# Expert blocks of 64 rows in one stationary tile, and the first two projection tiles of each norm multiplied together

## The reference, cut to what matters

```python
for l in range(2):                              # first stage
    xn = rms_norm(h, norm_mix[l]);  proj = xn @ w_in[l]
    ...                                         # recurrence and attention
    h = h + mix @ w_out[l]
    xn = rms_norm(h, norm_ffn[l]);  gu = xn @ w_ffn_in[l]
    h = h + (silu(gu[..., :D_FF]) * gu[..., D_FF:]) @ w_ffn_out[l]

h = rms_norm(x, g_mix) @ w_in                   # second stage
...
x = x + cross_attention(rms_norm(x, g_cross), ...)
hm = rms_norm(x, g_ffn)                         # [512, 1024]
group = argmax(hm @ w_group);  top 2 of the 8 experts of that group per token
for each expert e (of 32), rows xb routed to it:          # 1024 assignments in all
    yb = (silu(xb @ w_gate[e]) * (xb @ w_up[e])) @ w_down[e]   # 1024 -> 512 -> 1024
out = rms_norm(x + sum of a token's two yb * weight, g_final)
```

## Time and profile before

| | |
|---|---|
| time, median of 3 runs | 2981.32 us (2975.47 to 2982.77) |
| profiled execution, own time | 2980.58 us |
| its span | 2978.8 us |
| mean granted TensorE clock | 0.951 of full speed |
| PE busy | 2772.9 us, 93% |
| DVE / ACT / POOL busy | 1587.5 / 956.2 / 1142.2 us |
| DMA | 373.35 MB, mean 125 GB/s |

### The profile page before, as it was taken

One profiled execution on the slowest core, in us unless ns is written; L12 is line 12 of the kernel. 1 busy time (PEld: TensorE's weight loads), 2 busy tenths in 40 slices (PEclk: granted clock), 3 DMA queues, 4 the chain that ended last, 5 costly groups with the idle time before them and its releaser, 6 DMA issues.

```text
span 2978.8 us, 38117 instructions
## 1 busy us (share of the span) xinstructions
PE 2772.9 (93%) x12974; PEld 2209.5 (74%) x12974; DVE 1587.5 (53%) x2172; ACT 956.2 (32%) x1468; POOL 1142.2 (38%) x768
## 2 busy tenths in 40 slices
PE   6989899999998898999999999999889699999994
PEld 4768777887867787778878787875666488888883
DVE  4772664122355845641223433025644699999995
ACT  4322322110023313211110121122112477777775
POOL 4752016666757610066666563610250011111110
PEclk9999899999999998999999999969996899999997
DMA  3213002332322120023323222300131399999995
GB/s 130 66 36 93 1 22 85 99 98 85 92 72 65 49 71 29 1 85 99 96 88 115 78 88 82 106 29 1 38 117 44 124 356 363 356 371 367 364 361 192
DMA packets 82375, 373.35 MB, mean 125 GB/s; under 512 B 15440, under 2 KB 15568, under 8 KB 57552
## 3 DMA queue, kind: packets, MB, share of 16 engines
q1 hardware_dynamic: 71888, 360.23, 35.0%
q0 software_dynamic: 9504, 8.42, 0.9%
q10 hardware_dynamic: 864, 3.15, 0.3%
HBM read 376.97 MB, written 20.97 MB: 134 GB/s over the span
## 4 chain that ended last, share of the span: by engine, by line
PE 83%; DVE 8%; issue 3%; POOL 2%; ACT 2%; DMA 1%; DVEq 0%; ACTq 0%; SPq 0%; POOLq 0%
PE PS L1779 21%; PE PS L1780 20%; PE PS L1781 20%; PE PS L2126 6%; PE PS L2149 4%; PE PS L1893 2%; PE PS L2140 2%; PE PS L2086 2%; PE PS L1845 1%; PE PS L2204 1%; POOL arena L579 1%; POOL arena L578 1%; PE PS L1832 1%; DVE arena L1109 1%; DVE xl L1039 1%
## 5 line engine op out<-in xcount | busy, mean ns | idle before, releaser
L555 POOL TENSOR_SCALAR whi<-ring 128x1024 fp32r<-128x1024 f32 x260 | 291.8, 1122 | 1177.6 <-PE PS L1781 958.8
L558 POOL TENSOR_TENSOR wlo<-ring,whi 128x1024 fp32r<-128x1024 f32 x260 | 657.5, 2529 | 21.7
L1779 PE MATMUL PS<-xh,whi 128*128 128x512 f32 x1312 | 519.9, 396 | 15.1 <-POOL wlo L558 7.1
L1781 PE MATMUL PS<-xh,wlo 128*128 128x512 f32 x1312 | 512.4, 391 | 0.0
L1780 PE MATMUL PS<-xl,whi 128*128 128x512 f32 x1312 | 512.1, 390 | 0.0
L1779 PEld LDWEIGHTS PS<-xh,whi 128*128 128x128 f32 x1312 | 247.7, 189 | 71.6 <-issue 10.6
L1542 DVE TENSOR_TENSOR arena_r<-arena,arena_r 128x1024 fp32r<-128x1024 f32 x256 | 296.3, 1218 | 1.1 <-ACT arena_r L947 1.1
L1780 PEld LDWEIGHTS PS<-xl,whi 128*128 128x128 f32 x1312 | 247.9, 189 | 53.7 <-issue 2.9
L1781 PEld LDWEIGHTS PS<-xh,wlo 128*128 128x128 f32 x1312 | 247.2, 188 | 52.4
L947 ACT ACTIVATE arena_r<-arena 128x1024 fp32r<-128x1024 f32 x256 | 253.2, 1056 | 46.2 <-DMA arena<-w_gate 45.3
L1779 PE MATMUL PS<-xs,whi 128*128 128x512 f32 x560 | 232.2, 415 | 17.4 <-DVE xs L1217 10.1
(11 more groups left out here) (387 smaller groups left out, 4779.9 us busy)
## 6 DMA issues: line engine op xcount, KB each, us to landing
ring<-ring_w SPq DMA_DIRECT2D x280, 512.0 KB, 3.5
arena<-w_gate SPq DMA_DIRECT2D x64, 1024.0 KB, 6.8
arena<-w_up SPq DMA_DIRECT2D x64, 1024.0 KB, 6.8
arena<-w_down SPq DMA_DIRECT2D x64, 1024.0 KB, 6.7
arena<-y_dram SPq DMA_DIRECT2D x8, 512.0 KB, 7.0
xT<-xT_in SPq DMA_DIRECT2D x1, 2048.0 KB, 8.5
out<-arena SPq DMA_DIRECT2D x4, 512.0 KB, 2.6
arena<-memT_in SPq DMA_DIRECT2D x1, 1024.0 KB, 7.4
```

What stands on the lines that cost most here:

```text
L555: nc.gpsimd.tensor_scalar(whi[:, t % 2, :], ring[:, t % RING, :], 1.0, 0.0, ALU.mult, ALU.add).then_inc(sems["whi"], 1)
L558: nc.gpsimd.tensor_tensor(wlo[:, t % RING, :], ring[:, t % RING, :], whi[:, t % 2, :], ALU.subtract).then_inc(sems["split"], 1)
L1779: mm(out, a[0], b[0], start=start, stop=False)
L1781: return mm(out, a[1], b[0], start=False, stop=stop)
```

## The change

**Experts.** A block has `TB` = 64 rows; the number of overflow blocks goes from 8 to 16. `xgT` holds the high parts of the 64 transposed rows in columns 0 to 63 and their low parts in 64 to 127 of one stationary tile. A gate or up chunk is multiplied by two matmuls: that tile by the high part and by the low part of the weight; row r of the output then holds what came from the high part of row r, row 64 + r what came from its low part. ACT copies the two banks to `gsb` and `usb`. `turn_gu` takes the place of `turn_h`: eight plain float32 matmuls with a 128x64 matrix `fold` (ones at r and 64 + r) as the moving operand, which transpose and add the two halves. Silu and the product then work on 128x256 (`silu`, `hidden`). `down` has 64 stationary columns; for the first two quarters it does the three products as before, for the last two one plain float32 matmul per 512 columns, on the loaded floats, with no high and low part. The ACT and DVE orders of a block are changed to fit.

**Behind each norm.** `first_pair` replaces the waiting form of `feature_major`: it waits for the splits of both tiles and for the second chunk of `xh`, then per chunk multiplies both tiles by `xh` (four matmuls), then per chunk both by `xl` (two). In `late_norm` ACT makes the eight `xh` chunks first and the eight squares after them, and PE's sum of the squares moves from behind the second tile to behind the third.

**Routing** is adapted to 64-row blocks: two compare-and-add steps become one comparison against seven limits, the table has 50 blocks instead of 42, and the search for the expert of an overflow block goes over 16 instead of 8.

```diff
-OVER = 7
+TB = 64
+OVER = 15
...
+        xgT = [xh[:, 2 * u:2 * u + 2, :].rearrange("p a b -> p (a b)").rearrange("p (a b) -> p a b", b=P)
+               for u in range(2)]
...
@@ late_norm (ACT)
                     nc.scalar.activation(xh[:, c, :], xT[:, c, :], ACT.Identity, scale=lcol[:, C_FFN + c:C_FFN + c + 1]
                                          ).then_inc(sems["xh"], 1)
+                for c in range(KO):
                     nc.scalar.activation(sq8[:, c, :], xT[:, c, :], ACT.Square).then_inc(sems["sq"], 1)
...
@@ routing (DVE)
-            jj = E_[:, 0:8].unsqueeze(2).broadcast_to([P, 8, NEXP])
+            jj = E_[:, 0:16].unsqueeze(2).broadcast_to([P, 16, NEXP])
...
@@ projections (PE)
+            def first_pair(l, bank, t, high, low):
+                for j in range(2):
+                    pe.wait_ge(sems["split"], nth("split", l, t + j + 1))
                 for c in range(KO):
-                    pe.wait_ge(sems["xn"], nth("xn", l, (wait if wait_low is None else wait_low) + c + 1))
-                    ins = mm(out, whi[:, t % 2, c * P:c * P + P], xl[:, c, :], start=False, stop=(c == 7))
+                    pe.wait_ge(sems["xh"], nth("xh", l, high + max(c, 1) + 1))
+                    for j in range(2):
+                        for w in weights(t + j, slice(c * P, c * P + P)):
+                            mm(PS[:, bank + j, :], w, xh[:, c, :], start=(c == 0 and w.name == whi.name), stop=False)
+                for c in range(KO):
+                    pe.wait_ge(sems["xn"], nth("xn", l, low + c + 1))
+                    for j in range(2):
+                        ins = mm(PS[:, bank + j, :], whi[:, (t + j) % 2, c * P:c * P + P], xl[:, c, :],
+                                 start=False, stop=(c == 7))
+                        if c == 7:
+                            ins.then_inc(sems["tile"], 1)
...
@@ experts (PE)
-                        ins = mm3(PS[:, bank, :], [x[:, c, :] for x in xgT[u % 2]],
-                                  (high(w, k)[:, of], low(w, k)[:, of]),
-                                  start=(c == 0), stop=(c == 7))
+                        mm(PS[:, bank, :], xgT[u % 2][:, c, :], high(w, k)[:, of], start=(c == 0), stop=False)
+                        ins = mm(PS[:, bank, :], xgT[u % 2][:, c, :], low(w, k)[:, of], start=False, stop=(c == 7))
...
+                for j, buf in enumerate((gsb, usb)):
+                    for c in range(4):
+                        ins = mm(PS[:, 4, (4 * j + c) * TB:(4 * j + c) * TB + TB], buf[:, c * P:c * P + P], fold,
+                                 start=True, stop=True)
...
+                        if k < SPLIT_D:
+                            ins = mm3(out, [x[:, k, :] for x in hTs], (high("D", k)[:, of], low("D", k)[:, of]),
+                                      start=(k == 0), stop=False)
+                        else:
+                            ins = mm(out, hT[:, k, :], loaded("D", k)[:, of], start=(k == 0), stop=(k == 3))
```

More of the change, by code:

```diff
@@ L941, in _, with highs @@
             act_e.wait_ge(sems["h"], nth("h", DEPTH, 16))
-            def highs(w, i, u):
-                for k in range(4):
+            def highs(w, i, u, quarters=range(4)):
+                for k in quarters:
                     act_e.wait_ge(MS["w" + w][k // 2], lin(i, u, 16, 16))
@@ L1537, in _, with lows @@
             g4 = lg[:, :, 0:4]
-            def lows(w, i, u):
-                for k in range(4):
-                    v.wait_ge(MS["high" + w], lin(i, u, 4, k + 1))
+            def lows(w, i, u, quarters=range(4), each=4):
+                for k in quarters:
+                    v.wait_ge(MS["high" + w], lin(i, u, each, k + 1))
                     tt(low(w, k), loaded(w, k), high(w, k), ALU.subtract).then_inc(MS["low" + w], 1)
```

224 lines of the change are left out of this document (123 added, 101 removed).

## The result

| | before | changed |
|---|---|---|
| median, us | 2981.31 (2970.46 to 2984.73, 14 runs) | 2961.61 (2932.98 to 2975.11, 14 runs) |
| ratio, 95% interval | 1 | 0.9929 (0.9911 to 0.9947) |
| profiled execution, us (span) | 2980.58 (2978.8) | 2968.1 (2966.3) |
| PE idle ahead of the tiles' matmuls for POOL's low part (L558, now L568), us | 7.1 | 24.3 |

The change is 0.7% faster, 9.6 us above the forecast of 2952, and inside its range. The runs of the changed kernel lie 42 us apart, those of before 14. Part of that is PE's clock: the two lowest runs (2933.0 and 2934.9 us) were granted 0.960 of full speed on average, the other twelve 0.944 to 0.952. Those twelve still lie 24 us apart, so something else may happen in some executions and not in others.

A forecast was written before the change was run, and what follows sets the result against it. PE was taken to bound the expert stage, with the DMA engines close behind. 2980.58 - 42.6 (experts) + 13.4 (pairs) = 2951.4 us for the profiled execution, forecast as 2952 us, range 2934 to 2974.

The forecast's parts named there:

- The block, 16.8 us: Expert stage: PE's work sums to 16.6 us, 16.8 taken instead of 18.05; 30 distances give -37.5 us.
- The DMA engines: Expert stage: 6.5 MB a block would take 15.4 to 16 us and fit under 16.8.
- the burst of 424: Six first expert loads queued together moved 424 GB/s, 15.4 us a block; taken as evidence against a 358 GB/s bound.
- The rival with 17.5 us: Expert stage: DMA engines already full at 97% busy, block 17.5 us, gain 16.5 instead of 37.5, 2973 us; chance 10%.
- DVE's order as a bound: Expert stage: PE waits for each quarter of down, 0.5 us more a block, 17.3 us, total 2967; chance 8%.
- The rival in which the pairs gain 10 us: Behind the norms: POOL's split covered, five places give 2 us each, -10 instead of +13.4, 2929 us; chance 6%.
- Gathers and scatters halve; they are hidden behind the block and cost nothing either way: Expert stage: smaller row transfers on POOL would change the time by nothing.
- the experts' ends: First and last expert blocks: -1.8 us for the first reload, -3.7 for fewer last-block matmuls, -1 for its down.
- Slower: Expert stage: gaps of about 3 us waiting for loads, half clock behind, block 18.7 us, total 3009; chance 3%.
- Routing's +1.4: Ahead of the first gather: five DVE operations double their columns, +0.27 us each, other edits cancel to within 0.3.
- Pairs: Behind the norms: +3.8 and +3.3 us mixers, +5 feed-forwards, +2.3 second stage's first norm, -1 cross norm, together +13.4.
- the signs listed in advance: Expected traces, and wrong if the expert stage loses under 25 us or the part to 2306 grows under 5 or over 20.

The follow-up runs named there:

- split3: Changed kernel without pairs, POOL's copy of the scatter's row numbers earlier, three quarters of down split into fp32r parts instead of two: 2945.88 us, ratio 0.9866.
- split4: Changed kernel without pairs, POOL's copy of the scatter's row numbers earlier, all four quarters of down split, no plain float32: 2975.79 us, ratio 0.9976.
- split4_ahead: Changed kernel without pairs, all four quarters of down split, each gather issued a block earlier on POOL: 2925.70 us, ratio 0.9817.
- gather_ahead: Changed kernel with each gather issued a block earlier on POOL, behind it the scatter of two blocks before: 2952.21 us, ratio 0.9907.

## Why the prediction was right, and where not

**The block, 16.8 us: right**, and by its terms. In the trace after, the four plain float32 matmuls take 3.58 us (2520.85 to 2524.43; forecast 3.5), `turn_x` 0.93 (0.87), the folds 1.7 (1.9), and the other 44 matmuls the rest, 10.6 (10.3). split3 and split4, planned with the same prices, landed on 16.5 and 16.0.

**The DMA engines: right.** 390 GB/s, and 407 in split4_ahead, are both over the 358 that the Trainium skill ("DMA: Bandwidth & Descriptors", section on bandwidth) gives as the bound; the choice of the burst of 424 against it held. The rival with 17.5 us is out. So is DVE's order as a bound at two quarters (17.3 us). With four, the blocks that grow wait for loads through ACT and DVE, so there the DMA engines begin to count. The rival in which the pairs gain 10 us is out with them at 12 to 17 us of cost.

**"Gathers and scatters halve; they are hidden behind the block and cost nothing either way": this step failed.** That they move less was true, and it was beside the point. What the change moved is DVE: before, 2.9 us of waits and small work lay between its `y_v` (done at 2572.38) and its first quarter (2575.32), and POOL issued the scatter in them. From the timelines of DVE and POOL before:

```profile
2571.69 0.69 DVE L1730 COPY xT<-PS 128x512 f32<-128x512 f32 x1 [0.20 <-PE PS L1781]
...
2573.68 1.02 POOL L624 DMA_INDIRECT y_dram<-xT,idyi  x1 [0.88 <-POOL idyi L621]
```

Now the distance varies from block to block. In most blocks it is still over 1 us and the scatter gets in ahead; in the two with a hold the quarters of up follow after 0.85 us, and the scatter falls into them. This cost the profiled execution 16.1 us, and the median 9.4 (changed against gather_ahead; 7 by the ratios). That 9.4 nearly equals the 9.6 us by which the forecast was low is chance: two more parts were off, the experts' ends by 5.8 us the same way, and in the trace the part ahead of the experts by 5.4 us the other way. In the profiled execution, 16.7 us over its forecast of 2951.4, the sum is plain to within 0.2: 16.1 for the holds, 5.8 for the ends, less 5.4 because the part ahead of the first reload lost 9.4 us and not 14.8 (pairs and routing). The rival *Slower* had the second half of the mechanism, a gap and half clock behind it, but supposed it in each block and from the weights' loads.

**Experts' ends: 5.8 us too much.** From the first reload on, gather_ahead gains 38.2 us (615.9 to 577.7); the forecast had 37.5 + 1.8 + 3.7 + 1 = 44. The first distance fell from 13.5 to 11.5, as said. The second is 20.0, since PE waits 0.92 us for ACT's copy of up and 1.85 for a quarter behind ACT's first silu, whose table load takes 1.28 us; before, that load (at 2363.19) ended 1.25 us ahead of the silu, so nobody waited for it. And the tail, from the last gate load to the end, fell from 78.2 to 76.0 us, 2.2 in place of 4.7. Routing's +1.4 was met (first gather 12.2 us behind, matmuls ahead of it 10.8).

**Pairs: sign and sum right, terms not.** +13.4 was forecast; the two ways to measure them give 16.7 and 12.0 by the medians, 13 and 12 by the ratios. By place, forecast and trace: first mixer 3.8 and 3.7, second 3.3 and 2.0, feed-forwards 2.5 each and 5.3 and 5.5, the second stage's first norm 2.3 and 5.2, the cross norm -1.0 and -1.2, 20.5 in all. The three that came out 2.8 to 3.0 too low share a cause, PE's clock behind the bare split. In the second stage everything up to tile 2 went as forecast (it starts at 1725.19, by the forecast at 1710.0 plus the 15.1 us of delay so far); then thirteen matmuls run at 0.43 us in place of 0.23, 2.6 us. In the first feed-forward eight do so from 495.32 on, 1.6 us, and eight more at the pair's own start, which the forecast had as "1.4 more if the clock falls" and took half of. It had priced the gap ahead of a pair and forgotten the one behind. Behind the first mixer's pair the clock did not fall, and there the forecast was met. That the sum still came out near is luck: 15 us came back in the cross attention through the clock, of which no step had spoken, and 7 were lost the same way in the self attention.

**Of the signs listed in advance** one was missed. The forecast was to be wrong if the expert stage lost less than 25 us, and in the profiled execution it lost 21.9 from the first reload on (615.9 to 594.0), 23.3 from 2306 us on. The holds' 16.1 us are what is missing: gather_ahead, without their cost, loses 38.2. The others were there: 16.8 us, PE at 100%, 390 GB/s, PE idle 3.5 us after the pairs; the pair in the first feed-forward began at 477.53, which is 473.8 once the 3.7 us lost in the mixer are taken off, for 474; DVE's gate work (L1098, before L1074) started 5.0 us later, for 4. The part up to 2306 us grew by 10.8 us, inside 5 to 20.

## What to carry to other kernels

An indirect transfer issued by POOL is not free because its data is small: its issue can be shut out for as long as DVE runs operations with two SBUF inputs back to back, so after any change that tightens DVE look at the longest issue, not the median one, and give the gather a block of lead so that such a hold finds nobody waiting. When a reordering makes PE wait 3 us, price the clock behind the wait as well as the wait (0 to 2.6 us here). And where runs of a changed kernel spread more than those of before, compare their granted clocks first, then look for an event that occurs a varying number of times; a single trace shows its price.

## What the runs showed of the hardware

- A scatter's issue on POOL takes 0.92 us alone (1.02 in the 128-row form), up to 2 us when it begins inside one of DVE's quarters and gets in at its end, and 7.45 or 7.54, 7.69, 8.89, 14.38 or 14.64 us when it is held while DVE does not stop; each of the long ones ended 0.8 to 0.9 us after DVE fell idle or turned to an operation that reads PSUM.
- PE's clock fell to the lower level behind waits of 3.5 us and stayed there for some 3 us of matmuls in the first feed-forward, 7 us behind the 4.55 us wait of the long block, and for 27 to 68 us in attention stretches where PE was 92 to 100% busy by the records. Behind the wait of 3.62 us in the first mixer it did not fall. How long differed between kernels whose code there is the same: 27, 51 or 68 us in the self attention.
- The DMA engines carried 407 GB/s for 100 us beside full work on all engines.
